# New start addresses for the on-chip tensors of a two-block transformer kernel

## The chip, the cores and the metric

The kernel runs on one core of a Trainium2 chip. The metric is the device time of one execution in microseconds, the median of several runs. A core has TensorE (PE) for matmuls, VectorE (DVE), ScalarE (ACT), GpSimd (POOL) and SyncE (SP), here the engine that issues the weight loads. SBUF is the on-chip memory: every tensor in it has up to 128 partitions, and an address here is the byte offset within each partition, the same in all of them.

## The reference

All in float32, 256 tokens of width 2048, two layers in sequence:

```
h = rms_norm(x); p = h @ w_in                    # 2048 -> 6448 columns
y = concat(rwkv7_mixer(p), gated_delta_rule(p))  # 16 heads of 64, 8 heads of 128
x = x + y @ w_out
x = x + (silu(h2 @ w_gate) * (h2 @ w_up)) @ w_down      # width 5632
x = rms_norm(x)
x = x + fox_attention(rms_norm(x)) @ fox_w_out   # 16 heads of 128, causal
x = x + conv_ffn(rms_norm(x))                    # 2 x 5632 up, 3-tap convolution, silu gate, down
```

## The kernel before, in words

The activations lie transposed: a tile has 128 features as partitions and the 256 tokens along the row, so one tile is 256 x 4 = 1024 bytes of each partition. X, the residual, holds 16 such tiles. H holds the 16 normalised ones twice: H[:, 0] is the value cut to the matmul's short float (fp32r), H[:, 1] the rest. HID does the same for the 44 tiles of the hidden layer.

Weights stream through four slots. A unit of weights is 128 x 2048 floats (8192 bytes of each partition, 1 MB). SP loads it into slot u % 4 of RAW in two DMAs, once PE has used the unit that was there four before. ScalarE (`hi`, L505) writes the short part of the unit to HIW, which has two slots; VectorE (`lo`, L876) writes RAW minus HIW to LOW, which lies over RAW. PE (`unit`) then takes each weight tile of 128 x 128 floats, 512 bytes of each partition, and issues three matmuls of 256 columns that add up in a PSUM bank: HIW x H[:, 0] (L1578), HIW x H[:, 1] (L1579), LOW x H[:, 0] (L1580). A plain unit has 2 feature tiles times 8 output tiles (f = 0 to 7), so 48 matmuls. The stationary operand is the weight tile, at f x 512 bytes from the start of a slot's half; the moving operand is the H or HID tile. Every matmul has its own weight load, listed as PEld.

The order of the work is written out by hand, with semaphores: norm; input projection (six groups of 8 units); the two mixers with many small matmuls; output projection (two groups); gate and up projection (11 groups, `group_phase`); down projection (`down`, two halves of 22 units, moving operand HID); two norms; attention's projection (six groups), attention, its output projection, the second feed-forward. At the end of each half of a down or output projection PE stops until VectorE has added the sums to X and the next unit is cut. Squares for the norms are taken into NSQ; in the second feed-forward VectorE computes the convolution from UC, whose rows are 258 floats long, into YG and YV (L1537). PR holds the 51 tiles of the input projection, each 260 floats long, so 1040 bytes apart. In the delta rule's inversion (L1702 to L1712) the tensors gLO, gTM, gPM and gTT lie in the weight slots at multiples of 8192 bytes from w0, and each head's tile is 512 bytes.

SBUF addresses are also written out by hand at the top of `build`, as a running offset o that starts at 16512. Before, X lies first, then the weight slots (w0), then the small tables ident, ones, headones, vec (582 columns), small, causal and rstd, then H (h0), then the large region r2 that PR, NSQ, HID, QKV and the others share at different times. The masks lie at the region's end. YG and YV, used last, reach over the masks' place. Line numbers of the profile are those of the listing.

Of the kernel before, what the change touches and what calls it, by code (L numbers as in the profile page):

```python
# [20 lines left out]
ALU = mybir.AluOpType  # L21
ACT = mybir.ActivationFunctionType
AX_X = mybir.AxisListType.X

P = 128
T = 256
# [51 lines left out]
VEC_COLS = _c  # L78


def build(nc, io, out):
    with ExitStack() as ctx:
        sems, counts = {}, {}

        def S(name):
            if name not in sems:
                sems[name] = ctx.enter_context(nc.semaphore(name))
            return sems[name]

        def tick(ins, name, by=1):  # L90

            ins.then_inc(S(name), by)
            counts[name] = counts.get(name, 0) + by
            return counts[name]
# [10 lines left out]
        def own(engine, name):  # L105

            engine.wait_ge(S(name), counts[name])


        def at(name, shape, offset, dt=F32):  # L110
            return nc.alloc_sbuf_tensor_at(name, shape, dt, offset=offset)

        o = nc.sbuf_base if isinstance(nc.sbuf_base, int) else 0
        o = (o + 63) // 64 * 64
        base0 = o
        X = at("X", [P, KT, T], o); o += 16384
        w0 = o
        RAW = at("RAW", [P, RAW_SLOTS, UNIT], o)
        LOW = at("LOW", [P, RAW_SLOTS, UNIT], o, F32R); o += 32768
        HIW = at("HIW", [P, HI_SLOTS, UNIT], o, F32R); o += 16384  # L120
        ident = at("ident", [P, P], o); o += 512
        ones = at("ones", [P, P], o); o += 512
        headones = at("headones", [P, P], o); o += 512
        vec = at("vec", [P, VEC_COLS], o); o += (VEC_COLS * 4 + 63) // 64 * 64
        small = at("small", [P, 256], o); o += 1024
        causal = at("causal", [P, P], o); o += 512
        rstd = at("rstd", [P, T], o); o += 1024
        h0 = o
        H = at("H", [P, 2, KT, T], h0, F32R); o += 32768
        r2 = o  # L130
        end = base0 + 212800
        masks = end - 5632
        upper2 = at("upper2", [P, 2, P], masks)
        upper, upper_eq = upper2[:, 0, :], upper2[:, 1, :]
        lower1 = at("lower1", [P, P], masks + 1024)
        off = at("off", [P, 6, P], masks + 1536)
        chunk_go = at("chunk_go", [P, T], masks + 4608)
        assert r2 + 102192 <= masks and r2 + 90112 + 16600 <= end, (r2, masks, end)


        XIN = at("XIN", [P, NT, D], r2)
# [267 lines left out]
        def _(pool):  # L409
            def sel(dst, pattern, base, mult, op=ALU.is_ge, fill=0.0):  # L410
                tick(nc.gpsimd.affine_select(out=dst, in_=dst, compare_op=op, fill=fill, base=base,
                                             pattern=pattern, channel_multiplier=mult), "pool_step")
                own(pool, "pool_step")
# [14 lines left out]
                tick(nc.gpsimd.memset(off[:, i, :], 1.0), "pool_step")  # L428
            tick(nc.gpsimd.memset(upper, 1.0), "pool_step")
            tick(nc.gpsimd.memset(upper_eq, 1.0), "pool_step")  # L430
            tick(nc.gpsimd.memset(lower1[:], 1.0), "pool_step")
            tick(nc.gpsimd.memset(chunk_go[:], 1.0), "pool_step")
            own(pool, "pool_step")
            tick(nc.gpsimd.memset(chunk_go[:].rearrange("p (c t) -> p c t", t=C)[:, :, 0:1], 0.0), "pool_step")
# [2 lines left out]
                sel(off[:, i, :], [[m, P // m], [0, m]], m - 1, -1)  # L437
            sel(upper, [[1, P]], -1, -1)
            sel(upper_eq, [[1, P]], 0, -1)
            sel(lower1[:], [[-1, P]], -1, 1)  # L440

            tick(nc.gpsimd.memset(small[:, 80:144], 0.0), "pool_step")
            tick(nc.gpsimd.memset(causal[:], 0.0), "pool_step")
# [45 lines left out]
        def _(act):  # L489
            A = nc.scalar.activation  # L490

            def hi(u_const, g=None, step=0):

                lv = 32 * (u_const // 4 + 1)
                uv = u_const - HI_SLOTS + 1 + FREE_UNITS
                if g is not None:
                    lv = g * (8 * step) + lv
                    uv = g * step + uv
                if g is None and u_const < 4:
                    act.wait_ge(landed[u_const], 48)  # L500
                else:
                    act.wait_ge(landed[u_const % 4], lv + 16)
                act.wait_ge(unit_used, uv)
                n = unit_cols(u_const)
                A(HIW[:, u_const % 2, 0:n], RAW[:, u_const % 4, 0:n], ACT.Copy).then_inc(hi_made, 1)  # L505
# [22 lines left out]
            def squares(n0, half, dst=None):  # L528

                for f in range(8 * half, 8 * half + 8):  # L530
                    act.wait_ge(bank_freed, n0 + f + 1 + FREE_BANKS)
                    A((dst or NSQ)[:, f, :], X[:, f, :], ACT.Square).then_inc(S("squared"), 1)  # L532

            def root(k):
                act.wait_ge(S("variance"), k + 1)
                A(rstd[:], rstd[:], ACT.Sqrt).then_inc(S("rooted"), 1)
# [29 lines left out]
            for q in range(4):  # L566
                act.wait_ge(S("x_turned"), q + 1)
                A(X[:, 4 * q:4 * q + 4, 0:P], ps[q][:, :].rearrange("p (f t) -> p f t", f=4), ACT.Copy)\
                    .then_inc(S("x_tiles"), 1)
            act.wait_ge(S("x_tiles"), 8)  # L570
            for q in range(4):
                A(NSQ[:, 4 * q:4 * q + 4, :], X[:, 4 * q:4 * q + 4, :], ACT.Square).then_inc(S("squared"), 4)
            hi(0)
# [211 lines left out]
            for f in range(KT):  # L785
                act.wait_ge(S("x_scaled"), f + 1)
                A(NSQ[:, f, :], X[:, f, :], ACT.Square).then_inc(S("squared"), 1)
            root(3)
# [74 lines left out]
        def _(dve):  # L863
            V = nc.vector

            def step(ins):
                tick(ins, "dve_step")
# [35 lines left out]
            def norm(k, gain, eps, between=None):  # L903
# [3 lines left out]
                for e in range(9):  # L907
                    if e < 8:
                        for f in (2 * e, 2 * e + 1):
                            ins = V.scalar_tensor_tensor(NSQ[:, f, :], X[:, f, :], vec[:, c + f:c + f + 1], rstd[:],  # L910
                                                         ALU.mult, ALU.mult)
# [15 lines left out]
            for i, pack in enumerate(PACKS):  # L927
                r = sum(n for _, n in pack)
                dve.wait_ge(S("vecs_turned"), i + 1)
                V.tensor_copy(vec[:, c0:c0 + r], ps[i % 4][:, (i // 4) * P:(i // 4) * P + r])\  # L930
                    .then_inc(S("vecs_made"), 1)
                c0 += r
# [15 lines left out]
            dve.wait_ge(S("masks_made"), 1)  # L948
            step(V.tensor_tensor(upper, upper, off[:, 5, :], ALU.mult))
            step(V.tensor_tensor(upper_eq, upper_eq, off[:, 5, :], ALU.mult))  # L950
            step(V.tensor_tensor(lower1[:], lower1[:], off[:, 0, :], ALU.mult))
            step(V.tensor_copy(headones[:], off[:, 5, :]))
            settle()
            for i in range(5, -1, -1):
# [600 lines left out]
        def _(pe):  # L1555
# [82 lines left out]
            for i, pack in enumerate(PACKS):  # L1638
                r = sum(n for _, n in pack)
                if i >= 4:  # L1640
                    pe.wait_ge(S("vecs_made"), i - 3)
                nc.tensor.transpose(ps[i % 4][:, (i // 4) * P:(i // 4) * P + r], VPACK[0:r, i, :],
                                    ident[0:r, 0:r]).then_inc(S("vecs_turned"), 1)
# [424 lines left out]
```

## Time and profile before

| | |
|---|---|
| median of 3 runs | 2824.09 us (2810.8 to 2828.05) |
| profiled execution | 2826.51 us, its span 2824.8 us |
| mean granted clock of TensorE | 0.961 of full |
| TensorE busy, VectorE busy, ScalarE busy | 95%, 53%, 39% |
| bytes moved by DMA | 421.74 MB, mean 149 GB/s |

The span runs from the first to the last instruction. Matmuls overlap in the pipeline: one takes about 280 ns from start to end while the next starts after less than half of that, so the rate is read from how many start in a stretch of time.

### The profile page before, as it was taken

Reading aid. Unit: us, or ns where it says so; the run is one execution under the profiler, and the core shown is the slowest. Engines: PE = TensorE matmul, PEld = TensorE weight load, DVE = VectorE, ACT = ScalarE, POOL = GpSimd, SP = SyncE. Lnnn points to the kernel's source line nnn. Section 1 sums busy time; section 2 is a strip of 40 time slices with the busy share of each in tenths; the row PEclk is TensorE's granted clock in tenths of the full one; section 3 lists DMA queues with packets and bytes.
Section 4 is the critical chain, followed back from the end, with each engine's and each line's share of the span. In section 5 each row is a group of like instructions: output and inputs, shape, how many; then the busy total and the mean of one; then the engine's idle time right before and its main releaser. Section 6 shows DMA issues by size and latency. Waiting matters only on the chain.

```text
span 2824.8 us, 57090 instructions
## 1 busy us (share of the span) xinstructions
PE 2690.9 (95%) x24185; PEld 2611.7 (92%) x24185; DVE 1496.0 (53%) x1680; ACT 1108.8 (39%) x1050; POOL 67.9 (2%) x71
## 2 busy tenths in 40 slices
PE   7999988888999999999999799998999999999999
PEld 6999778487989999999999799977989999999999
DVE  5457556474454444444444544546466666565444
ACT  3333323232344444443333333434344445454332
POOL 1000130000000000000010000000100000000000
PEclk9999989588999999999999899988999999999999
DMA  5555200001545555555555455520545555555654
GB/s 170 185 189 182 74 3 4 1 1 61 169 156 181 190 182 190 182 188 183 188 185 160 131 185 186 185 90 15 184 157 180 190 182 190 182 189 183 188 184 149
DMA packets 169214, 421.74 MB, mean 149 GB/s; under 512 B 17462, under 2 KB 22139, under 8 KB 168859
## 3 DMA queue, kind: packets, MB, share of 16 engines
q1 hardware_dynamic: 168699, 419.13, 45.7%
q8 instruction: 76, 1.25, 0.2%
q10 hardware_dynamic: 416, 1.18, 0.1%
q14 instruction: 23, 0.19, 0.0%
HBM read 418.16 MB, written 2.10 MB: 149 GB/s over the span
## 4 chain that ended last, share of the span: by engine, by line
PE 89%; DVE 8%; ACT 2%; issue 1%; SPq 0%; DMA 0%; DVEq 0%; POOL 0%; ACTq 0%; POOLq 0%
PE ps L1578 26%; PE ps L1580 25%; PE ps L1579 25%; DVE LOW L876 1%; PE ps L1618 1%; PE ps L1998 1%; DVE NSQ L910 1%; ACT HIW L505 1%; PE ps L1675 1%; PE ps L1668 1%; PE ps L1702 1%; PE ps L1712 1%; PE ps L1731 1%; PE ps L1709 1%; PE ps L1966 0%
## 5 line engine op out<-in xcount | busy, mean ns | idle before, releaser
L876 DVE TENSOR_TENSOR LOW<-RAW,HIW 128x2048 fp32r<-128x2048 f32 (+2 forms) x400 | 910.9, 2278 | 1082.0 <-ACT HIW L505 1081.8
L1578 PE MATMUL ps<-H,HIW 128*128 128x256 f32 x4928 | 1387.1, 281 | 42.5 <-DVE LOW L876 20.6
L1579 PE MATMUL ps<-H,HIW 128*128 128x256 f32 x4928 | 1382.1, 280 | 0.0
L1580 PE MATMUL ps<-H,LOW 128*128 128x256 f32 x4928 | 1381.1, 280 | 0.0
L505 ACT ACTIVATE HIW<-RAW 128x2048 fp32r<-128x2048 f32 (+2 forms) x400 | 759.2, 1899 | 1263.3 <-PE ps L1580 1263.3
L1578 PEld LDWEIGHTS ps<-H,HIW 128*128 128x128 f32 x4928 | 932.6, 189 | 46.7 <-issue 26.1
L1580 PEld LDWEIGHTS ps<-H,LOW 128*128 128x128 f32 x4928 | 932.4, 189 | 0.0
L1579 PEld LDWEIGHTS ps<-H,HIW 128*128 128x128 f32 x4928 | 929.7, 189 | 0.0
L1578 PE MATMUL ps<-HID,HIW 128*128 (+1 forms) x1408 | 393.0, 279 | 0.8 <-DVE LOW L876 0.8
L1579 PE MATMUL ps<-HID,HIW 128*128 (+1 forms) x1408 | 391.8, 278 | 0.0
L1580 PE MATMUL ps<-HID,LOW 128*128 (+1 forms) x1408 | 391.8, 278 | 0.0
L1578 PEld LDWEIGHTS ps<-HID,HIW 128*128 128x128 f32 x1408 | 264.3, 188 | 1.0 <-DVE LOW L876 1.0
L1580 PEld LDWEIGHTS ps<-HID,LOW 128*128 128x128 f32 x1408 | 264.6, 188 | 0.0
L1579 PEld LDWEIGHTS ps<-HID,HIW 128*128 128x128 f32 x1408 | 263.5, 187 | 0.0
L1537 DVE SCALAR_TENSOR_TENSOR YG<-UC,vec,YG 128x256 f32<-128x256 f32 x88 | 42.0, 478 | 0.0
L1537 DVE SCALAR_TENSOR_TENSOR YV<-UC,vec,YV 128x256 f32<-128x256 f32 x88 | 42.0, 477 | 0.0
L845 ACT ACTIVATE UC<-ps 128x256 f32<-128x256 f32 x88 | 30.6, 384 | 14.6 <-PE ps L1580 14.6
L482 POOL TENSOR_TENSOR NSQ<-NSQ 128x1024 f32<-128x1024 f32 (+1 forms) x4 | 11.3, 2819 | 933.1 <-ACT NSQ L532 933.0
L541 ACT ACTIVATE H<-NSQ 128x512 fp32r<-128x512 f32 x32 | 20.2, 631 | 31.0 <-DVE NSQ L910 31.0
L1675 PE MATMUL ps<-rstd,ident 16*64 16x256 f32 (+1 forms) x80 | 18.9, 595 | 13.8 <-DVE rstd L1022 13.8
L1675 PEld LDWEIGHTS ps<-rstd,ident 16*64 16x64 f32 (+1 forms) x80 | 10.4, 219 | 21.4 <-DVE rstd L1022 15.3
L626 ACT ACTIVATE gPM<-ps 128x512 f32<-128x512 f32 x20 | 11.9, 597 | 43.8 <-PE ps L1702 43.8
(354 smaller groups left out, 1800.5 us busy)
## 6 DMA issues: line engine op xcount, KB each, us to landing
RAW<-in_ffn_w_up SPq DMA_DIRECT2D x264, 512.0 KB, 4.5
RAW<-in_ffn_w_down SPq DMA_DIRECT2D x176, 512.0 KB, 4.8
RAW<-in_w_in SPq DMA_DIRECT2D x96, 512.0 KB, 4.1
RAW<-in_fox_w_in SPq DMA_DIRECT2D x96, 512.0 KB, 4.3
RAW<-in_ffn_w_gate SPq DMA_DIRECT2D x88, 512.0 KB, 3.8
RAW<-in_w_out SPq DMA_DIRECT2D x32, 512.0 KB, 4.9
RAW<-in_fox_w_out SPq DMA_DIRECT2D x32, 512.0 KB, 4.9
RAW<-in_w_in SPq DMA_DIRECT2D x4, 576.0 KB, 4.8
```

The source lines that it names most:

```text
L505: A(HIW[:, u_const % 2, 0:n], RAW[:, u_const % 4, 0:n], ACT.Copy).then_inc(hi_made, 1)
L845: A(UC[:, i, 2:2 + T], ps[i][:, 0:T], ACT.Copy).then_inc(bank_freed, 1)
L876: V.tensor_tensor(LOW[:, u_const % 4, 0:n], RAW[:, u_const % 4, 0:n], HIW[:, u_const % 2, 0:n].bitcast(F32), ALU.subtract).then_inc(lo_mad ...
L910: ins = V.scalar_tensor_tensor(NSQ[:, f, :], X[:, f, :], vec[:, c + f:c + f + 1], rstd[:], ALU.mult, ALU.mult)
L1537: ins = V.scalar_tensor_tensor(y(i), UC[:, i, j:j + T], tap(g, j, i), y(i), ALU.mult, ALU.add)
L1578: mm(o_, hi_w, h_hi, start=start, stop=False)
L1579: mm(o_, hi_w, h_lo, start=False, stop=False)
L1580: i = mm(o_, lo_w, h_hi, start=False, stop=stop)
L1618: i = mm(ps[0][:, 0:T], ones[:], sq[:, f, :], start=f == (8 if presummed else 0), stop=f == KT - 1 and not presummed)
L1668: ins = mm(ps[b0][0:16, 0:T], sel[:, c:c + 16], src[:, f, :], start=f == 0, stop=f == tiles - 1)
L1675: ins = mm(ps[b0 + f // 2][e * n:(e + 1) * n, (f % 2) * T:(f % 2 + 1) * T], ident[0:16, h:h + 1].broadcast_to([16, n]), rstd[0:16] if buf ...
L1702: ins = mm(ps[2 * b][:, (h % 4) * P:(h % 4 + 1) * P], LO[:, h, :], TM[:, h, :], start=True, stop=True)
```

## The change

X, the weight slots (RAW, LOW, HIW), H and the region r2 with all in it now begin on multiples of 1024 bytes. For that the tables ident, ones, headones, rstd and vec go ahead of X, after which the offset is rounded up to the next multiple of 1024 (from 21400 to 21504). small, cut from 256 to 192 columns, and causal go into the region r2, at 102208 bytes from its start, and the masks right behind. lower1, a mask that nothing reads, is removed, with its memset, its select and its multiplication. No other instruction changes but for its addresses.

```diff
@@ build
+        ident = at("ident", [P, P], o); o += 512
+        ones = at("ones", [P, P], o); o += 512
+        headones = at("headones", [P, P], o); o += 512
+        rstd = at("rstd", [P, T], o); o += 1024
+        vec = at("vec", [P, VEC_COLS], o); o += VEC_COLS * 4
+        o = (o + 1023) // 1024 * 1024
         X = at("X", [P, KT, T], o); o += 16384
         w0 = o
         RAW = at("RAW", [P, RAW_SLOTS, UNIT], o)
         LOW = at("LOW", [P, RAW_SLOTS, UNIT], o, F32R); o += 32768
         HIW = at("HIW", [P, HI_SLOTS, UNIT], o, F32R); o += 16384
-        ident = at("ident", [P, P], o); o += 512
-        ones = at("ones", [P, P], o); o += 512
-        headones = at("headones", [P, P], o); o += 512
-        vec = at("vec", [P, VEC_COLS], o); o += (VEC_COLS * 4 + 63) // 64 * 64
-        small = at("small", [P, 256], o); o += 1024
-        causal = at("causal", [P, P], o); o += 512
-        rstd = at("rstd", [P, T], o); o += 1024
         h0 = o
         H = at("H", [P, 2, KT, T], h0, F32R); o += 32768
         r2 = o
         end = base0 + 212800
-        masks = end - 5632
+        small = at("small", [P, 192], r2 + 102208)
+        causal = at("causal", [P, P], r2 + 102208 + 768)
+        masks = r2 + 102208 + 1280
         upper2 = at("upper2", [P, 2, P], masks)
         upper, upper_eq = upper2[:, 0, :], upper2[:, 1, :]
-        lower1 = at("lower1", [P, P], masks + 1024)
-        off = at("off", [P, 6, P], masks + 1536)
-        chunk_go = at("chunk_go", [P, T], masks + 4608)
-        assert r2 + 102192 <= masks and r2 + 90112 + 16600 <= end, (r2, masks, end)
+        off = at("off", [P, 6, P], masks + 1024)
+        chunk_go = at("chunk_go", [P, T], masks + 4096)
+        assert h0 % 1024 == 0 and masks + 5120 <= end and r2 + 90112 + 16600 <= end, (r2, masks, end)
@@ gpsimd
-            tick(nc.gpsimd.memset(lower1[:], 1.0), "pool_step")
...
-            sel(lower1[:], [[-1, P]], -1, 1)
@@ vector
-            step(V.tensor_tensor(lower1[:], lower1[:], off[:, 0, :], ALU.mult))
```

## Rows read from the trace of the kernel before

**Rows 1.** The page, busy time, share of the span and instructions of each engine.
```profile
PE 2690.9 (95%) x24185; PEld 2611.7 (92%) x24185; DVE 1496.0 (53%) x1680; ACT 1108.8 (39%) x1050; POOL 67.9 (2%) x71
```
**Rows 2.** The page, the chain that ended last, by engine and by line.
```profile
PE 89%; DVE 8%; ACT 2%; issue 1%; SPq 0%; DMA 0%; DVEq 0%; POOL 0%; ACTq 0%; POOLq 0%
PE ps L1578 26%; PE ps L1580 25%; PE ps L1579 25%; DVE LOW L876 1%; PE ps L1618 1%; PE ps L1998 1%; DVE NSQ L910 1%; ACT HIW L505 1%; PE ps L1675 1%; PE ps L1668 1%; PE ps L1702 1%; PE ps L1712 1%; PE ps L1731 1%; PE ps L1709 1%; PE ps L1966 0%
```
**Rows 3.** The page, costliest groups (busy, mean ns | idle before, releaser).
```profile
L876 DVE TENSOR_TENSOR LOW<-RAW,HIW 128x2048 fp32r<-128x2048 f32 (+2 forms) x400 | 910.9, 2278 | 1082.0 <-ACT HIW L505 1081.8
L1578 PE MATMUL ps<-H,HIW 128*128 128x256 f32 x4928 | 1387.1, 281 | 42.5 <-DVE LOW L876 20.6
...
L505 ACT ACTIVATE HIW<-RAW 128x2048 fp32r<-128x2048 f32 (+2 forms) x400 | 759.2, 1899 | 1263.3 <-PE ps L1580 1263.3
...
L1578 PE MATMUL ps<-HID,HIW 128*128 (+1 forms) x1408 | 393.0, 279 | 0.8 <-DVE LOW L876 0.8
```
**Rows 4.** Windows: from:to, length, busy time (records) by engine, clock, DMA share, GB/s.
```profile
56.00:250.00 194.00, 194.00 (x1649) 194.00 (x1649) 104.64 (x117) 69.76 (x40) 0.00 (x0) 1.00 0.55 185
1000.00:1200.00 200.00, 200.00 (x1701) 200.00 (x1700) 91.14 (x56) 87.58 (x64) 0.00 (x0) 1.00 0.57 185
1437.80:1550.00 112.20, 112.20 (x990) 112.20 (x990) 46.57 (x22) 38.21 (x21) 3.98 (x2) 1.00 0.55 176
1966.00:2003.00 37.00, 36.79 (x324) 36.80 (x325) 13.30 (x6) 11.51 (x6) 0.00 (x0) 1.00 0.53 162
2500.00:2690.00 190.00, 190.00 (x1616) 190.00 (x1615) 101.52 (x88) 77.03 (x57) 0.00 (x0) 1.00 0.59 187
604.00:638.00 34.00, 34.00 (x307) 34.00 (x306) 22.35 (x37) 8.41 (x15) 0.00 (x0) 1.00 0.01 1
```
**Rows 5.** The chain in order of time, after two stops: start, length.
```profile
1437.80 0.38 PE ps L1578
1438.18 0.11 PE ps L1579
...
2016.68 0.38 PE ps L1578
...
2017.18 0.12 PE ps L1580
```
**Rows 6.** Timeline of PE in the first gate and up projection: start, length.
```profile
900.11 0.28 PE L1578 MATMUL ps<-H,HIW 128*128 128x256 f32 x1
...
900.46 0.28 PE L1578 MATMUL ps<-H,HIW 128*128 128x256 f32 x1
...
900.81 0.28 PE L1578 MATMUL ps<-H,HIW 128*128 128x256 f32 x1
```
**Rows 7.** Views of single tiles (PR, UC, X): ns min/median/max, first and last start.
```profile
L964 DVE COPY PR<-ps x48: 408/414/426, 99.4 to 327.0; 128x256 f32 x24, 128x256 f32<-128x256 f32 x24
...
L1537 DVE SCALAR_TENSOR_TENSOR YG<-UC,vec,YG x88: 472/478/482, 2119.0 to 2579.1; 128x256 f32<-128x256 f32 x88
...
L910 DVE SCALAR_TENSOR_TENSOR NSQ<-X,vec,rstd x64: 472/477/485, 30.5 to 2075.0; 128x256 f32<-128x256 f32 x64
```
**Rows 8.** What SP's queue waited for, and DMA issues (KB, us to landing).
```profile
SPq L301 <- PE ps L1580: 1928.6, 392, 106.8
...
RAW<-in_ffn_w_up SPq DMA_DIRECT2D x264, 512.0 KB, 4.5
...
XIN<-in_x SPq DMA_DIRECT2D x2, 1024.0 KB, 8.2
```
**Rows 9.** Timeline of POOL and DVE around lower1.
```profile
5.04 0.20 POOL L431 MEMSET lower<- 128x128 f32 x1
...
12.32 0.29 POOL L411 TENSOR_SCALAR_AFFINE_SELECT lower<-lower 128x128 f32<-128x128 f32 x1
...
59.54 0.28 DVE L951 TENSOR_TENSOR lower<-lower,off 128x128 f32<-128x128 f32 x1
...
63.47 2.29 DVE L876 TENSOR_TENSOR LOW<-RAW,HIW 128x2048 fp32r<-128x2048 f32 x1 [0.22 <-DVE off L958]
```

## The prediction

> **What bounds the kernel now.** I read the page's busy shares first [rows 1]: TensorE is busy 95% of the span, VectorE 53%, ScalarE 39%. The chain of waits says the same more sharply: PE is 89% of what ended last, and its lines 1578, 1579 and 1580, the three matmuls of every weight tile, are 26%, 25% and 25% of the span [rows 2]. Then the costliest groups [rows 3]: (4928 + 1408) × 3 = 19008 such matmuls of 256 columns. ScalarE's cut of the weights (L505) spends its idle time waiting for PE, and VectorE's (L876) for ScalarE, so both run ahead of PE's need. The DMA queue spends 1928.6 us waiting until PE has used a slot [rows 8]. So in the streamed phases neither data nor a helper engine is late, and the span is the number of matmuls times their spacing, plus short hand-overs between phases.
>
> So the question is what sets the spacing, and whether addresses can. From the stretches [rows 4], taking two records off each count for those cut by the edges: 194 us / 1648 = 117.7 ns, 200 / 1699 = 117.7, 190 / 1614 = 117.7, but 112.2 / 988 = 113.6 in the second half of the first down projection, and PE's 36.79 / 322 = 114.3 in the first half of the second output projection (384 matmuls; the two make up some 1400). The granted clock is 1.00 (2.4 GHz) in all of them. There are thus two levels, some 4.2 ns apart, at the same clock. The hand-overs show when a level is picked [rows 5]: both down halves and both output halves read the same tiles by the same code from the same residues, but after its stop before 1437.80 us PE goes on in short steps (a second step of 0.11 us), and after a like stop before 2016.68 us in longer ones (0.12). From then on the stretch keeps its level until the next stop. The level is therefore not fixed by the addresses alone; it is picked anew at each restart, and the difference between runs (2810.8 to 2828.05 us) is about what one long phase at the other level would give: 4224 matmuls of a gate/up phase × 4.2 ns = 18 us.
>
> **The change part by part.** Residues mod 1024, worked out from the offsets in the code, which start at byte 16512. Before: X, RAW/LOW and HIW at 128; H and everything in the big region, HID too, at 448. After: all at 0.
>
> Weight tiles. A stationary tile is 512 bytes. Before it starts at 128 for even f and at 640 for odd f, and the odd one runs over a multiple of 1024. In the timeline the triples of even and odd f alternate, and their starts are 0.35 us apart each time [rows 6]: 128 or 640, crossing or not, costs nothing that shows. After, the residues are 0 and 512, none crosses. Taken: 0.
>
> Moving tiles. H and HID tiles are 1024 bytes, start at 448 and cross one multiple of 1024, always; after, never. The trace has no fp32r matmul with a moving tile that doesn't cross, so this must be bounded. Nearest row: the inversion's matmuls at full clock, whose tiles cross or don't by the head's parity, run at 34 us / 305 = 111.5 ns throughout [rows 4]. They are fp32 and read half as many bytes per ns. Bound on the good side: all fast, 111.5 ns: 17600 × 6.2 ns (those at 117.7) + 1400 × 2.1 ns (those at 113.6) = 112 us less. Bound on the bad side: moving and stationary tiles were 320 bytes apart mod 512; afterwards they are 0 apart, and if PE's two readers then meet, one step between levels more: 17600 × 4.2 + 1400 × 8.3 = 86 us more. I take 0, since the rows nearest in kind (the two levels at one set of addresses, the parity of f) show no dependence on the address. That the other engines are busy or not doesn't matter either: VectorE is busy 46% of the stretch at 1000 us, 54% of that at 56 us, and the spacing is the same [rows 4].
>
> VectorE and ScalarE. The projections' tiles in PR are 1040 bytes apart, so the 48 copies of L964 write at all multiples of 16; they take 408 to 426 ns [rows 7]. L1537 reads UC shifted by 4 and 8 bytes and takes 478 ns; L910, with its operands 64-byte aligned, 477 [rows 7]. So X, NSQ, UC, YG and the weight cuts change by 0, within ±3 ns each; were it 3 ns on all 400 cuts, that would be 1.2 us of VectorE time under PE's cover, which costs nothing.
>
> DMA. Weights land at 128 mod 256 before and at 0 after. A shorter landing than the 4.5 us of [rows 8] frees nobody, since PE's use of slots is what the queue waits for. The one landing that PE waits for is x, 8.2 us from issue [rows 8], at most 5% of it: 0.4 us. Taken: 0. The Trainium skill ("DMA: Bandwidth & Descriptors", How a descriptor splits into AXI transactions) gives a descriptor that doesn't start on 256 bytes one extra transaction, so a 4096-byte row would need 17 instead of 16. By it the transfers get a few per cent shorter; the sum stays, by the queue's wait.
>
> lower1. Gone are one VectorE multiplication, 0.28 us at 59.5 us, and on GpSimd a memset of 0.20 and a select of 0.29 us [rows 9]. VectorE's lies under PE's work: its next cut of weights begins at 63.47 us, 0.22 us after it could have [rows 9], and PE is busy without a gap from 56 us on [rows 4]. GpSimd's are done by 13 us, and the product that reads lower1 runs at 59.54. Without that cover it would be 0.28 us. small and causal move to where nothing of the same time lies (FQ ends at 102112 above the region's start, small begins at 102208); no wait is added, no step moved past a queue.
>
> The sum: 2826.5 (the profiled run; its span is 2824.8) − 0 to 0.5. It lies 2.4 us above the median, which is a matter of the level picked, so I put the forecast at the median, 2824.
>
> **The rivals.** (a) The alignment decides the level, and every restart gets 113.6: 17600 × 4.2 = 74 us less, 2750. For it: the slower level has something to lose, and the crossing of 1024 by every moving tile is the thing the change removes in full. Against: 113.6 is already reached with the crossing there.
> (b) The stall of the array goes wholly: 111.5 ns, 2712. For it: the fp32 rows at 111.5. Against: these stream at half the rate. The Trainium skill ("TensorE: Matmul & The Clock Gate", Back-to-back issue gap) gives N/2.4 + 2.5 ns for a warm matmul, 109.2 for 256 columns; by an estimate from that page the kernel would reach 2824 − 156 = 2668. The trace disagrees with it for these pairs by 4.4 to 8.5 ns, and nothing there ties this to the address.
> (c) Slower: moving and stationary tile now start at the same residue, and the weight load, which runs while the matmul of before streams, is held by it on each tile: +86 us, 2910. It decides only if the readers share a resource narrower than 1024 bytes. Against: the inversion pairs tiles of one residue with each other (gLO with gTM) and still runs at 111.5.
> (d) The change doesn't do what it says: X's offset would have to miss a multiple of 1024. The code rounds up and asserts H's, so I give it nothing of its own; its time would be that of the forecast.
>
> **How the numbers follow.** Forecast (no dependence, level picked at restarts): 0.62, its own range 2802 (the best run, 2810.8, less half of the 18 us that one long phase is worth) to 2836 (all restarts at 117.7: 2826.5 + 1400 × 4.2 ns = 2832, and run scatter). (a) 0.16; (b) 0.06; (c) 0.12; the rest, 0.04, is a partial shift of levels, half to either side. The range from 2740 to 2836 takes in the forecast's and (a), with half of the rest: 0.80. Within 1% (±28 us, about what a measurement of this kernel can tell from no change) is the forecast alone, 0.62; faster by more (a), (b) and half the rest, 0.24; slower 0.14.
>
> **What the profile after would show.** Stretches of the dense phases with 117.7 and 113.6 ns in another mix, and VectorE's 2278 ns of L876 and L1537's 478 unchanged [rows 3, 7], say the steps are right. One level only, in every dense stretch, says an alignment rule exists: 113.6 or less (a), 111.5 (b), above 120 (c). A changed landing time with unchanged spacing says DMA cares and the kernel doesn't. I would be wrong if the spacing depends on moving tiles crossing multiples of 1024 or on the distance of the two operands, neither of which varies for fp32r in this trace.

## The result

The changed kernel takes 2873.05 us (median of 4 runs, 2872.35 to 2874.73) against 2825.11 (4 runs, 2810.8 to 2828.05): a ratio of 1.0181, 95% interval 1.0146 to 1.0216. It is slower by 1.8%, where no change was forecast. Ratios compare only runs within 1.5% of the fastest of their kernel; where the kernel before had very short runs, most of its others fall outside, and there the medians over all runs stand beside the ratio.

The page of the changed kernel, first the busy line, then the chain by line and the costliest groups (all line numbers are 2 or 3 lower than before, since lower1's lines are gone), to be held against [rows 1 to 3]:

```profile
PE 2739.4 (95%) x24185; PEld 2661.3 (93%) x24185; DVE 1497.5 (52%) x1679; ACT 1108.8 (39%) x1050; POOL 63.2 (2%) x69
...
PE 89%; DVE 8%; ACT 2%; issue 1%; SPq 0%; DMA 0%; DVEq 0%; POOL 0%; ACTq 0%; POOLq 0%
...
L874 DVE TENSOR_TENSOR LOW<-RAW,HIW 128x2048 fp32r<-128x2048 f32 (+2 forms) x400 | 910.9, 2277 | 1123.6 <-ACT HIW L503 1123.2
L1575 PE MATMUL ps<-H,HIW 128*128 128x256 f32 x4928 | 1403.1, 285 | 40.8 <-DVE LOW L874 18.9
...
L503 ACT ACTIVATE HIW<-RAW 128x2048 fp32r<-128x2048 f32 (+2 forms) x400 | 758.4, 1897 | 1306.3 <-PE ps L1577 1306.2
...
L1575 PEld LDWEIGHTS ps<-H,HIW 128*128 128x128 f32 x4928 | 952.9, 193 | 44.8 <-issue 26.1
```

The number of matmuls and the shares of the chain are the same; the cut on VectorE takes 2277 ns as before (2278). What has grown is PE's busy time, by 48.5 us, that of its weight loads with it, and the idle time of the helpers behind it. The idle time ahead of L1575 is no larger (40.8 us, 42.5 before), so nothing new is waited for. The stretches say where it went, in windows of the changed kernel (length, busy time and records by engine, clock, DMA share, GB/s), to be held against [rows 4]:

```profile
61.00:250.00 189.00, 189.00 (x1577) 189.00 (x1577) 98.58 (x106) 66.90 (x38) 0.00 (x0) 1.00 0.54 181
1000.00:1200.00 200.00, 200.00 (x1669) 200.00 (x1668) 93.72 (x60) 89.22 (x70) 0.00 (x0) 1.00 0.56 183
1465.00:1575.00 110.00, 110.00 (x919) 110.00 (x918) 43.56 (x19) 36.37 (x19) 0.00 (x0) 1.00 0.51 167
1999.00:2049.00 50.00, 50.00 (x419) 50.00 (x418) 20.01 (x16) 17.96 (x16) 3.00 (x2) 1.00 0.54 168
2500.00:2700.00 200.00, 200.00 (x1669) 200.00 (x1668) 113.68 (x114) 86.27 (x69) 0.00 (x0) 1.00 0.56 180
615.00:648.00 33.00, 33.00 (x298) 32.98 (x296) 23.17 (x38) 7.16 (x12) 0.00 (x0) 1.00 0.00 1
```

With two records off each count as before: 189 / 1575, 200 / 1667, 110 / 917, 50 / 417, all 120.0 ns, at the full clock of 2.4 GHz. There were two levels, 117.7 ns and the prediction's 113.6 (away from the restart, from 1465 to 1535 us, it is 113.3); now there is one, in every phase, and also in the second half of the first down projection and the first half of the second output projection, which had been at the faster one. The sum closes to about 1 us: 17600 × 2.3 ns + 1400 × 6.4 ns = 49 us, and the span has grown by 48.2 us. The last row is the inversion's fp32 matmuls: 33 / 296 = 111.5 ns, exactly as before.

The rest of the argument held in the main. Single tiles (PR, X) and the DMA issues of the changed kernel, against [rows 7, 8]:

```profile
L961 DVE COPY PR<-ps x48: 414/417/426, 101.1 to 333.1; 128x256 f32 x24, 128x256 f32<-128x256 f32 x24
...
L908 DVE SCALAR_TENSOR_TENSOR NSQ<-X,vec,rstd x64: 476/484/495, 31.4 to 2109.6; 128x256 f32<-128x256 f32 x64
...
SPq L301 <- PE ps L1577: 1977.8, 392, 105.4
...
RAW<-in_ffn_w_up SPq DMA_DIRECT2D x264, 512.0 KB, 4.4
...
XIN<-in_x SPq DMA_DIRECT2D x2, 1024.0 KB, 8.1
```

These two landings are 0.1 us shorter; among the other loads some are shorter and some longer, by 0.1 to 0.3 us. The queue waits 49 us longer for PE: it is PE that is slower, and DMA has more room than before.

VectorE, ScalarE and DMA read and write the weight slots too. That none of them sets the spacing can be read within one stretch. From 1000 to 1200 us of the changed kernel, with a triple counted from every matmul, 250 triples ran while both engines were idle all along, and 127 while both were busy for over 90% of the time: the spacing is 120.0 ns in either. It is 120.0 as well in the 494 triples during which no DMA packet was under way, and in the 614 with at least 14 of them all along. In the kernel before it is 117.8 in all four (by the starts themselves; the windows, with two records off, give 117.7).

### The profile page after: what moved, and what is told of

The parts are those of the page before. It is cut to its first block, busy times and chain, and to the rows that moved or that the text cites. A ratio compares the mean times of both kernels' runs of the same rounds, so it can differ in the third digit from the quotient of the medians.

```text
span 2873.0 us, 57087 instructions
## 1 busy us (share of the span) xinstructions
PE 2739.4 (95%) x24185; PEld 2661.3 (93%) x24185; DVE 1497.5 (52%) x1679; ACT 1108.8 (39%) x1050; POOL 63.2 (2%) x69
## 4 chain that ended last, share of the span: by engine, by line
PE 89%; DVE 8%; ACT 2%; issue 1%; SPq 0%; DMA 0%; DVEq 0%; POOL 0%; ACTq 0%; POOLq 0%
PE ps L1575 26%; PE ps L1577 26%; PE ps L1576 26%; DVE LOW L874 1%; PE ps L1615 1%; PE ps L1995 1%; DVE NSQ L908 1%; PE ps L1672 1%; ACT HIW L503 1%; PE ps L1699 1%; PE ps L1665 1%; PE ps L1709 1%; PE ps L1728 1%; PE ps L1706 0%; PE ps L1963 0%
## 5 line engine op out<-in xcount | busy, mean ns | idle before, releaser
L874 DVE TENSOR_TENSOR LOW<-RAW,HIW 128x2048 fp32r<-128x2048 f32 (+2 forms) x400 | 910.9, 2277 | 1123.6 <-ACT HIW L503 1123.2
L1575 PE MATMUL ps<-H,HIW 128*128 128x256 f32 x4928 | 1403.1, 285 | 40.8 <-DVE LOW L874 18.9
L1576 PE MATMUL ps<-H,HIW 128*128 128x256 f32 x4928 | 1400.9, 284 | 0.0
L1577 PE MATMUL ps<-H,LOW 128*128 128x256 f32 x4928 | 1400.5, 284 | 0.0
L1575 PEld LDWEIGHTS ps<-H,HIW 128*128 128x128 f32 x4928 | 952.9, 193 | 44.8 <-issue 26.1
L1576 PEld LDWEIGHTS ps<-H,HIW 128*128 128x128 f32 x4928 | 953.0, 193 | 0.0
L1577 PEld LDWEIGHTS ps<-H,LOW 128*128 128x128 f32 x4928 | 952.7, 193 | 0.0
L1575 PE MATMUL ps<-HID,HIW 128*128 (+1 forms) x1408 | 398.6, 283 | 0.6 <-DVE LOW L874 0.6
L1576 PE MATMUL ps<-HID,HIW 128*128 (+1 forms) x1408 | 398.5, 283 | 0.0
L1577 PE MATMUL ps<-HID,LOW 128*128 (+1 forms) x1408 | 398.4, 283 | 0.0
L1575 PEld LDWEIGHTS ps<-HID,HIW 128*128 128x128 f32 x1408 | 270.3, 192 | 0.8 <-DVE LOW L874 0.8
L1577 PEld LDWEIGHTS ps<-HID,LOW 128*128 128x128 f32 x1408 | 270.3, 192 | 0.0
L1576 PEld LDWEIGHTS ps<-HID,HIW 128*128 128x128 f32 x1408 | 270.3, 192 | 0.0
```

The lines of the kernel that those rows point to most:

```text
L874: V.tensor_tensor(LOW[:, u_const % 4, 0:n], RAW[:, u_const % 4, 0:n], HIW[:, u_const % 2, 0:n].bitcast(F32), ALU.subtract).then_inc(lo_mad ...
L1575: mm(o_, hi_w, h_hi, start=start, stop=False)
L1576: mm(o_, hi_w, h_lo, start=False, stop=False)
L1577: i = mm(o_, lo_w, h_hi, start=False, stop=stop)
```

## The experiments

All use the new order of tensors, except where said. The edits are pads ahead of X, ahead of H and ahead of the large region r2, and the assertion on H's address is dropped. "Distance" is the address of the moving tile less that of the stationary one; since the stationary tiles lie at even and odd multiples of 512 bytes, it is only given modulo 512. The kernel before has 320, for H and HID; the changed one has 0. Where a kernel has a single run, its stretches are read, and not a difference of a few us.

**Are the residues the cause, and which?** Four kernels. The first gives the changed kernel its old residues:

```diff
         o = (o + 1023) // 1024 * 1024
+        o += 128
         X = at("X", [P, KT, T], o); o += 16384
...
+        o += 320
         h0 = o
```

The second has only the pad of 128, the third only a pad of 320 ahead of H, the fourth only one of 64 there.

> The changed kernel in its new order of tensors, but with the residues mod 1024 of the kernel before: weight slots at 128, H and the large region at 448. If residues are the cause, whichever: 117.7 ns a matmul in the dense stretches (some at 113.6) and 2811 to 2830 us. If the new order or the absolute place is the cause (rival): 120.0 ns and 2873 us.

> Weight slots, H and the large region all at residue 128. Distance between moving and stationary tile is the cause (theory): it is 0 as in the changed kernel, so 120.0 ns, 2873 us. Rival, the residue of the moving tile itself (it starts on a multiple of 1024 or doesn't cross one) or that of the weights: 117.7 ns or less, 2811 to 2830 us.

> Weight slots at 0, H and the large region at 320, so the distance of 320 of the kernel before. Distance theory: 117.7 ns (some 113.6), 2811 to 2830 us. Rival, the weights' residue 0 is what costs: 120.0 ns, 2873 us. Rival, the moving tile's own residue 0: also 117.7 here, told apart by the run with both at 128.

> Weight slots at 0, H and the large region at 64. If a distance of 64 mod 128 or mod 256 (which 320 also is) is what the kernel before had right: 117.7 ns, 2811 to 2830 us. If the distance counts mod 512 or 1024: another level, not foreseen, between 111.5 and 122 ns.

Measured: 2828.55 us (median of 10 runs; ratio to the kernel before 1.0014, 0.9976 to 1.0052), and, one run each, 2874.08, 2830.49 and 2825.54 us. The same window of the four, in that order, then the first dense stretch of the fourth:

```profile
1000.00:1200.00 200.00, 200.00 (x1700) 200.00 (x1700) 92.20 (x56) 87.82 (x64) 0.00 (x0) 1.00 0.57 186
```
```profile
1000.00:1200.00 200.00, 200.00 (x1669) 200.00 (x1668) 93.00 (x60) 89.23 (x69) 0.00 (x0) 1.00 0.56 182
```
```profile
1000.00:1200.00 200.00, 200.00 (x1701) 200.00 (x1700) 92.68 (x56) 87.38 (x64) 0.00 (x0) 1.00 0.58 187
```
```profile
100.00:240.00 140.00, 140.00 (x1238) 140.00 (x1237) 79.13 (x84) 53.08 (x31) 0.00 (x0) 1.00 0.58 195
1000.00:1200.00 200.00, 200.00 (x1700) 200.00 (x1700) 91.91 (x56) 89.26 (x65) 0.00 (x0) 1.00 0.57 186
```

That is 117.8, 120.0, 117.7 and 117.8 ns. The old residues give the old time in the new order, within 0.5% by the interval, so the move of the tables ahead of X is not what costs. With both operands at 128, where the moving tile starts off a multiple of 1024 and crosses one, it is 120.0: at equal residues neither the crossing nor the multiple matters. (A moving tile that doesn't cross, at another distance, wasn't run.) With the weights at 0, just where the changed kernel has them, and H elsewhere, it is 117.7: nor does the weights' own residue. What all of them agree with is the distance. The fourth also ran its input projection at 140 / 1236 = 113.3 ns, a phase that the kernel before ran at 117.7: at one set of addresses both levels turn up, in one phase or another.

**What is the period?** Four kernels with two distances each, one for the phases that read H, one for the down projections, which read HID in r2; for instance

```diff
+        o += 256
         h0 = o
         H = at("H", [P, 2, KT, T], h0, F32R); o += 32768
+        o += 128
         r2 = o
```

and in the same way 128 and 448, 32 and 192, 96 and 512.

> Weight slots at residue 0 throughout these four runs. H at a distance of 256, the large region with HID at 384. Theory: only equal places collide, so 117.7 ns (with restarts at 113.6) in the H stretches and in the down projections. Rival, the readers collide whenever the distance is a multiple of 128 or of 256: 120.0 ns in the H stretches (and, for 128, in the down projections too).

> H at 128, HID at 448. Theory (only equal places collide): 117.7 or 113.6 ns in both. Rival, period 128: 120.0 ns with H and 117.7 or 113.6 with HID. A third outcome, that some distance lets all matmuls go at 113.6 or 111.5, is open for both.

> H at 32, HID at 192. If the place that collides is 64 bytes wide or more: 120.0 ns with H. If it is 32 bytes or less: 117.7 or 113.6. HID at 192 (64 mod 128): 117.7 or 113.6 by every theory.

> H at 96, HID at 512. The weight tiles of odd f start at 512, those of even f at 0. Theory: a distance of 512 is the same as 0, as every second tile shares it in the changed kernel too, so 120.0 ns in the down projections; with H 117.7 or 113.6. Rival, a period of 1024 with only half the tiles colliding would alternate with f in both this and the changed kernel.

Measured, one run each: 2866.31, 2834.46, 2803.57 and 2874.26 us. The windows of the four, one stretch with H and the two halves of the first down projection:

```profile
1000.00:1200.00 200.00, 200.00 (x1669) 200.00 (x1669) 92.38 (x58) 88.18 (x65) 0.00 (x0) 1.00 0.56 183
1330.00:1410.00 80.00, 80.00 (x677) 80.00 (x676) 32.09 (x14) 27.14 (x15) 0.00 (x0) 1.00 0.57 185
```
```profile
1000.00:1200.00 200.00, 200.00 (x1687) 200.00 (x1687) 92.58 (x57) 87.14 (x63) 0.00 (x0) 1.00 0.57 185
1330.00:1410.00 80.00, 80.00 (x708) 80.00 (x707) 32.85 (x16) 28.83 (x15) 0.00 (x0) 1.00 0.59 193
```
```profile
1000.00:1200.00 200.00, 200.00 (x1717) 200.00 (x1716) 92.29 (x56) 88.28 (x64) 0.00 (x0) 1.00 0.57 187
1330.00:1410.00 80.00, 80.00 (x682) 80.00 (x681) 32.94 (x15) 26.80 (x14) 0.00 (x0) 1.00 0.58 187
1465.00:1535.00 70.00, 70.00 (x621) 70.00 (x620) 29.81 (x13) 24.27 (x14) 0.00 (x0) 1.00 0.56 183
```
```profile
1000.00:1200.00 200.00, 200.00 (x1669) 200.00 (x1668) 93.36 (x60) 89.33 (x69) 0.00 (x0) 1.00 0.56 183
1330.00:1410.00 80.00, 80.00 (x669) 80.00 (x668) 32.65 (x16) 26.81 (x14) 0.00 (x0) 1.00 0.56 181
```

My theory of these four, that only equal places collide, fell with the first: at 256 it is 120.0 ns, as at 0, while 128 and 384 give 118.7 and 118.5, 64 and 320 share their two levels, and so do 192 and 448. The levels repeat after 256 bytes and not after 128 or less. Nor is the rest one level: 96 gives 120.0 as well, where 117.7 or 113.6 was expected, and 32 gives 116.6. The 120.0 at 96 isn't quite the 120.0 of distance 0, though. From 1000 to 1200 us of the changed kernel every single step from start to start is 120 ns; with H at 96 the three steps of a triple are 118, 120 and 122 ns in the mean.

Two phases of these kernels need a second look: the second output projection of the one with H at 128, and the second gate and up projection of the one with H at 32:

```profile
1970.00:2018.00 48.00, 48.00 (x402) 48.00 (x401) 19.29 (x16) 17.96 (x16) 2.35 (x1) 1.00 0.54 171
```
```profile
2100.00:2300.00 200.00, 200.00 (x1700) 200.00 (x1699) 133.18 (x162) 100.89 (x91) 0.00 (x0) 1.00 0.56 184
```

So 128 has a second level too, 48 / 400 = 120.0 ns, and 32 has one of 200 / 1698 = 117.8.

**Does the distance alone do it, in the old kernel?** The kernel before, in its old order and with lower1, and one pad:

```diff
         rstd = at("rstd", [P, T], o); o += 1024
+        o += 192
         h0 = o
```

> The kernel before, in its old order and with lower1, and only a pad of 192 bytes ahead of H: weight slots stay at 128, H and the large region go from 448 to 640 mod 1024, a distance of 512. Distance theory with period 256: 120.0 ns in every dense stretch and 2873 us, a ratio of 1.017 to 1.018. Rival, something else in the new layout has a share (tables ahead of X, small and causal in the large region): less than that, down to 1.00.

Measured: 2868.44 us (4 runs, 2867.57 to 2869.04), ratio 1.0142 (1.0117 to 1.0167). Its windows:

```profile
61.00:250.00 189.00, 189.00 (x1578) 189.00 (x1577) 98.80 (x103) 66.90 (x38) 0.00 (x0) 1.00 0.54 183
1000.00:1200.00 200.00, 200.00 (x1669) 200.00 (x1668) 92.13 (x56) 86.88 (x64) 0.00 (x0) 1.00 0.56 184
```

120.0 ns again: 192 bytes ahead of H, and nothing else, make most of the loss, 1.4 of 1.8%. The ratio of 1.017 to 1.018 that was expected lies just outside the interval. The changed kernel, which wasn't timed side by side with this one, is 4.6 us longer. That is not in the dense stretches, whose spacing is the same. Of the 7.2 us between the two profiled spans, 4.2 lie between the end of the input projection and the end of the output projection's first half: 432.8 us in the changed kernel, 428.6 here. It is 428.7 in the kernel with H at 256, which has the new order and 120.0 ns as well, so the new order alone doesn't make it. The mean granted clock over the span is 0.965 here and 0.961 in the changed kernel, so part of it may be time that the mixers spent at 1.2 GHz; what makes the rest stays open. By the sum above the dense stretches alone should add 49 us to the kernel before here too, and the span has grown by 41.0: the time outside them moves by several us from kernel to kernel, and that the changed kernel's 48.2 us came so close to the sum is in part luck.

**The two distances left.** Pads of 224 ahead of H and 192 ahead of r2, and of 160 and 64:

> Weight slots at 0, H at 224, the large region with HID at 160 mod 256, the two multiples of 32 not seen yet. If the levels go by the distance mod 256: one steady level between 113.3 and 119 ns for each, not 120.0. If a small distance ahead is what helps (32 gave 116.7), 224 is no different from 192: 117.8 or 113.3.

> The two swapped: H at 160, HID at 224. If the level is a matter of the distance alone and not of the phase of the kernel, the H stretches show what the down projections of the run before showed and the other way round.

Measured, one run each: 2840.61 and 2830.48 us. The windows of the two; the third line of each is the phase in which the level at 160 was another one:

```profile
1000.00:1200.00 200.00, 200.00 (x1693) 200.00 (x1692) 91.62 (x56) 87.57 (x64) 0.00 (x0) 1.00 0.57 185
1330.00:1410.00 80.00, 80.00 (x684) 80.00 (x683) 33.30 (x15) 26.85 (x14) 0.00 (x0) 1.00 0.57 188
1465.00:1535.00 70.00, 70.00 (x592) 70.00 (x591) 27.94 (x13) 24.18 (x13) 0.00 (x0) 1.00 0.57 184
```
```profile
1000.00:1200.00 200.00, 200.00 (x1707) 200.00 (x1706) 91.11 (x56) 88.35 (x64) 0.00 (x0) 1.00 0.57 185
1330.00:1410.00 80.00, 80.00 (x678) 80.00 (x677) 32.11 (x14) 27.36 (x15) 0.00 (x0) 1.00 0.57 185
1650.00:1850.00 200.00, 200.00 (x1688) 200.00 (x1687) 94.10 (x76) 75.77 (x46) 0.00 (x0) 1.00 0.56 184
```

224 gives 118.3 ns with H (200 / 1691) and 118.3 with HID (80 / 676); 160 gives 117.3 with H (200 / 1705) and 117.3 with HID (80 / 682), and 118.6 in other phases of both (200 / 1686, 70 / 590), so it has two levels where one was expected. The swap shows what the pair was made for: the levels go with the distance, not with the phase of the kernel.

All distances in one table, each from windows as above:

| distance mod 256 | ns a matmul | seen at |
|---|---|---|
| 0 | 120.0 | 0 and 256 with H, 0 and 512 with HID, all phases |
| 32 | 116.6 or 117.7 | 32, both levels in each of two executions |
| 64 | 117.7 or 113.3 | 64, 320 |
| 96 | 120.0 | 96 |
| 128 | 118.6; 120.0 in one phase, the second output projection | 128, 384; 120.0 at 128 alone |
| 160 | 117.3 or 118.6 | 160, 416 |
| 192 | 117.6 or 113.3 | 192, 448 |
| 224 | 118.3 | 224, in two kernels |

**Which pair of operands?** The short parts H[:, 0] and the rests H[:, 1] are read by different matmuls, so they can be put at different distances:

```diff
+        o += 64
         h0 = o
-        H = at("H", [P, 2, KT, T], h0, F32R); o += 32768
+        H0 = at("H0", [P, KT, T], h0, F32R)
+        H1 = at("H1", [P, KT, T], h0 + 16384 + 192, F32R); o += 32768
...
+        o += 192
         r2 = o
...
-        COLS = at("COLS", [P, NT, P], h0 + 24576)
+        COLS = at("COLS", [P, NT, P], h0 + 24576 + 192)
```

with H[:, 0] and H[:, 1] taken from H0 and H1 throughout; and the opposite, H0 at 0 and H1 and r2 64 further.

> H split in two: the short parts H[:, 0] at a distance of 64 from the weight slots, the rests H[:, 1] at a distance of 0 (mod 256). If a weight load is slowed by the moving tile that streams at the same time, the step that is long is the one from L1576 to L1577 (rests stream, LOW loads), the other two are short. If a matmul is slowed by the distance to its own weights, the long step is from L1575 to L1576, as L1576 alone reads the rests. If only the mean distance counts, all three are alike. HID at a distance of 0: 120.0 ns in the down projections.

> The opposite: H[:, 0] at 0, H[:, 1] and HID at 64. If concurrent streams collide: the step from L1576 to L1577 is the short one and the two others are long. If a matmul and its own weights: the step into L1576 is the short one. In the down projections 117.8 or 113.3 ns.

Measured: 2854.01 and 2865.03 us, one run each. The costliest groups of the stretch from 1000 to 1200 us, busy time and mean ns of one, in the first kernel (H[:, 1] at distance 0) and in the second (H[:, 0] at 0). In each the three lines follow each other as L1575, L1576 and L1577 do in the changed kernel; they are L1583 to L1585 in the first and L1582 to L1584 in the second:

```profile
L1584 PE MATMUL ps<-H,HIW 128*128 128x256 f32 x561 | 159.9, 285 | 0.0
L1585 PE MATMUL ps<-H,LOW 128*128 128x256 f32 x562 | 157.1, 280 | 0.0
L1583 PE MATMUL ps<-H,HIW 128*128 128x256 f32 x562 | 156.5, 278 | 0.0
```
```profile
L1582 PE MATMUL ps<-H,HIW 128*128 128x256 f32 x556 | 158.5, 285 | 0.0
L1583 PE MATMUL ps<-H,HIW 128*128 128x256 f32 x557 | 158.2, 284 | 0.0
L1584 PE MATMUL ps<-H,LOW 128*128 128x256 f32 x556 | 156.2, 281 | 0.0
```

The first speaks for the load that runs beside the stream: the matmul whose moving tile lies at 0, L1584, is the long one, and from its start to that of the next it is 122 ns, against 117 to 118 for the two other steps; the mean spacing is 200 / 1683 = 118.8 ns. The second doesn't bear it out: the matmul that reads the tile at 64, L1583, is as long as the first, with a step of 122 ns behind it where the short one was expected, and the short step, 118 ns, is the one behind the last, whose tile lies at 0; the mean is the full 120.0. Nor does a matmul's own weight tile explain it: the step into L1583 is 120 to 121 ns there and not the short one. The three are not alike in either, so a mean distance isn't what counts, but neither of the two pairings explains both kernels. Each kernel also had a second level at the same addresses: 117.7 in a later phase of the first (200 / 1698, from 1650 us on) and 40 / 340 = 117.6 in the first output projection of the second (720 to 760 us). Which pair collides stays open. The down projections did as expected: 120.0 ns in the first kernel, with HID at 0, and 117.7 in the second, with HID at 64.

**A version that beats both?** The kernel with H at 32 and HID at 192 had the shortest single run, so it was timed.

> The addresses of the run with H at 32 and HID at 192, now timed against the kernel before. 13248 matmuls with H at 116.67 ns and 5632 with HID at 117.78 or 113.33 would give 2795 to 2815 us, a ratio of 0.990 to 0.996. Rival: the 116.67 ns was one pick among levels, as at a distance of 64, and the ratio is 0.998 to 1.002.

Measured: median 2804.22 us (12 runs, 2796.3 to 2810.93) against 2827.81 for the kernel before (17 runs, 2781.62 to 2836.36). Over all runs that is 0.8% less by the medians; the ratio as defined above is 1.0029 (0.9989 to 1.0070), not the 0.990 to 0.996 expected, since it keeps only the 5 shortest of the 17 runs of the kernel before. Both are true: the kernel before had 2 runs shorter than any of this one, and 14 longer than any of this one. That its short runs are those whose phases picked the faster levels is likely but not shown: there is no trace of a short run. Two windows of the timed kernel:

```profile
100.00:240.00 140.00, 140.00 (x1191) 140.00 (x1191) 75.26 (x80) 51.61 (x30) 0.00 (x0) 1.00 0.55 185
1000.00:1200.00 200.00, 200.00 (x1717) 200.00 (x1716) 93.11 (x56) 88.46 (x64) 0.00 (x0) 1.00 0.58 189
```

117.7 and 116.6 ns: the rival, that 116.6 was one pick among levels, came true, though the levels of 32 lie close together. A version that is faster than the kernel before beyond its scatter isn't shown.

## Why the prediction was wrong

**What bounds the kernel** was right: the span is the number of matmuls times their spacing, and the 48.2 us are, in the main, 19000 spacings that grew.

**The step that failed** is that of the moving tiles, "I take 0". It had two supports. One was the parity of f, whose two start addresses cost the same. That is true, but they are 512 bytes apart, twice the period, so the row could not have shown a dependence with a period of 256 or less; I read it as saying that nothing depends on addresses. The other was that two levels occur at one set of addresses. That is true as well, and still holds: a distance of 64 gives 117.7 or 113.3, picked anew after a stop. But the picking is among levels which the distance allows, and with all moving tiles at a distance of 0 only 120.0 was ever seen. "Not fixed by the addresses alone" was right and was then used as if it said "not by the addresses". In place of the 0 that was taken, the term measured 49 us. The prediction's last paragraph names the distance of the two operands as what would make it wrong, and as never varied in the trace; the sum put it at nothing all the same.

**The rival that came true** is (c), slower by the equal residues, with a chance of 0.12, and the upper end of 2836 left it out. Its condition is borne out: what counts is where the two operands of PE lie to each other, with a period narrower than 1024 bytes, namely 256. Its way of working, a weight load held by the matmul that streams beside it, isn't: of the two kernels with H split it fits one and not the other. Its price was mis-sized: one step between levels, 4.2 ns, was taken, and it was 2.3 ns on the 17600 matmuls and 6.4 on the 1400, 49 us and not 86. Against it stood the inversion, which pairs tiles of equal residue at 111.5 ns. Its distance is 0 before and after, and 111.5 may be its slow level as well as its only one: a row with a single distance could tell nothing of what the distance does, and for these fp32 matmuls no run here does.

**The bound below**, that never crossing a multiple of 1024 could help, found no support: the kernel with both operands at 128 crosses, and has the very 120.0 ns of the one that doesn't. **Rivals (a) and (b)** fell with it: no dense stretch of the changed kernel came near 113.6 or 111.5 ns.

**VectorE, ScalarE, DMA, lower1** were right to cost nothing: copies to PR take 417 ns (414), the cuts 2277 (2278), and PE's wait for the cuts is no longer than before (18.9 us ahead of L1575, 20.6 before). L908 takes 484 ns (477), over the 3 ns that I allowed. The extra transaction that the Trainium skill ("DMA: Bandwidth & Descriptors", How a descriptor splits into AXI transactions) gives a row off a multiple of 256 bytes may have a part in the two landings that are 0.1 us shorter; no run here tells that apart, and no time hung on it.

**The Trainium skill** ("SBUF — State Buffer", Who interferes with whom) gives PE two independent read ports, one for the moving operand and one for the weight load, and says that PE waits on nobody. Here the spacing is 117.7 or 113.3 ns at a distance of 64 between just these two operands and 120.0 at 0, with nothing else changed, so for fp32r pairs of 128 weight columns and 256 moving ones the measurement decides against it.

## What to carry to other kernels

In a stream of fp32r matmuls of 256 columns, each with its own weight load of 128, keep the start of the moving tile away from that of the stationary one modulo 256 bytes: 0 and 96 were the worst distances here, 32, 64 and 192 the best. Only steps of 32 bytes were tried, and only with this shape. Rounding every tensor to a large power of two makes that distance 0, which is the one to avoid. And before an address is called harmless because two of them cost the same, see by how much they differ: two samples a whole number of periods apart say nothing of what lies between.

## What the runs showed of the hardware that was not expected

The spacing of a steady stream of these matmuls takes a few sharp values at the same full clock: 113.3, 116.6, 117.3, 117.7, 118.3, 118.6 and 120.0 ns. Which of them are open is set by the distance mod 256, and where several are, one is picked when PE starts again after a stop, or when it goes over to moving tiles at another distance, and kept until the next such point, for up to some 5000 matmuls in the kernel before. I take that pick to be what spread the kernel before over 2781.62 to 2836.36 us in 17 runs: with 120.0 as the only level, 4 runs of the changed kernel lay within 2.4 us. That is an inference: there is no trace of a short run.
